# Attention of a two-layer hybrid transformer: three rotating PSUM banks for the turned probabilities, one bank for the weighted values, and the latent turn ahead of the scores

## What is computed

```python
def attend(q, k, v, scale):
    s = jnp.einsum('bqhd,bkhd->bhqk', q, k).astype(jnp.float32) * scale
    p = jax.nn.softmax(s, axis=-1).astype(v.dtype)
    return jnp.einsum('bhqk,bkhd->bqhd', p, v)

ya_x = blocked_attention(qa_x, concat([ka_c, ka_x]), concat([va_c, va_x]), MLA_SCALE)
yb_x = neighborhood_attention(qb_x, kb_x, vb_x, kb_c, vb_c, na_rpb, rows)
if need_ctx:                     # layer 0 only
    ya_c = attend(qa_c, ka_c, va_c, MLA_SCALE)
    yb_c = attend(qb_c, kb_c, vb_c, NA_SCALE)
```

## Time and profile before

| what | value |
|---|---|
| median of 3 runs | 2893.85 us (2892.34 to 2894.07) |
| the profiled execution | 2889.44 us, its span 2887.6 us |
| PE busy | 2807.2 us (97%) |
| DVE busy | 1482.7 us (51%) |
| ACT busy | 947.4 us (33%) |
| POOL busy | 263.3 us (9%) |
| PE in the chain that ended last | 89% |
| granted TensorE clock, mean | 0.996 of full speed |

### The profile page before, as it was taken

The page is one execution under the profiler, slowest core; times in us unless marked ns, Lnnn a source line. Parts: engine busy times, 40 slices in busy tenths (PEclk is TensorE's granted clock), DMA queues, the critical chain, the costliest instruction groups (busy, mean ns, idle before and its releaser), DMA issues.

```text
span 2887.6 us, 42480 instructions
## 1 busy us (share of the span) xinstructions
PE 2807.2 (97%) x16327; PEld 2646.7 (92%) x16327; DVE 1482.7 (51%) x2293; ACT 947.4 (33%) x1526; POOL 263.3 (9%) x279
## 2 busy tenths in 40 slices
PE   7999999999988899999999999999999998999999
PEld 5999999989977789999999999999998987888887
DVE  6554355455477665533553555245346587633332
ACT  3221122233388642211222322112224388532231
POOL 1000000031234210000000100000003234000000
PEclk9999999999999999999999999999999999999999
DMA  6433243223100224322442234133223201233333
GB/s 224 135 122 99 82 137 122 82 63 78 32 14 12 79 74 134 124 85 81 137 133 58 88 117 134 55 123 117 72 65 87 58 14 46 81 95 107 90 100 90
DMA packets 361092, 262.99 MB, mean 91 GB/s; under 512 B 11086, under 2 KB 339188, under 8 KB 359952
## 3 DMA queue, kind: packets, MB, share of 16 engines
q1 hardware_dynamic: 359440, 256.86, 29.5%
q10 hardware_dynamic: 896, 4.46, 0.4%
q0 software_dynamic: 640, 0.09, 0.0%
HBM read 255.08 MB, written 2.10 MB: 89 GB/s over the span
## 4 chain that ended last, share of the span: by engine, by line
PE 89%; ACT 4%; DVE 3%; issue 2%; POOL 1%; DMA 0%; SPq 0%; POOLq 0%; ACTq 0%; DVEq 0%
PE pair L427 24%; PE pair L428 24%; PE pair L435 24%; PE pair L1311 2%; PE pair L1313 2%; PE pair L1312 2%; PE pair L682 2%; PE pmid L2109 2%; PE pair L683 2%; PE pair L684 2%; ACT prob L2180 1%; ACT pt_hi L2165 1%; DVE pt_lo L2254 1%; PE psum L2134 1%; PE psum L2136 1%
## 5 line engine op out<-in xcount | busy, mean ns | idle before, releaser
L427 PE MATMUL pair<-h_lo,w_hi 128*128 128x384 f32 (+1 forms) x2656 | 906.4, 343 | 0.7 <-ACT sg L1102 0.4
L428 PE MATMUL pair<-h_hi,w_hi 128*128 128x384 f32 (+1 forms) x2656 | 905.4, 343 | 0.0
L427 PEld LDWEIGHTS pair<-h_lo,w_hi 128*128 128x128 f32 x2656 | 498.5, 188 | 22.8 <-issue 0.6
L428 PEld LDWEIGHTS pair<-h_hi,w_hi 128*128 128x128 f32 x2656 | 498.8, 188 | 21.3
L403 DVE TENSOR_TENSOR w_lo<-w_raw,w_hi 128x1024 fp32r<-128x1024 f32 (+1 forms) x262 | 349.0, 1332 | 324.5 <-ACT w_hi L396 321.3
L435 PE MATMUL pair<-h_hi,w_lo 128*128 128x384 f32 (+1 forms) x2656 | 513.8, 343 | 0.0
L435 PEld LDWEIGHTS pair<-h_hi,w_lo 128*128 128x128 f32 x2656 | 463.4, 188 | 20.6
L396 ACT ACTIVATE w_hi<-w_raw 128x1024 fp32r<-128x1024 f32 (+1 forms) x262 | 296.2, 1131 | 539.8 <-PE pair L435 507.4
L427 PE MATMUL pair<-s_lo,w_hi 128*128 128x384 f32 (+1 forms) x1100 | 377.7, 343 | 0.0
L428 PE MATMUL pair<-s_hi,w_hi 128*128 128x384 f32 (+1 forms) x1100 | 377.2, 343 | 0.0
L949 DVE SCALAR_TENSOR_TENSOR pmid<-mod_raw,cs_rows 128x1024 f32<-128x1024 f32 x256 | 315.3, 1232 | 74.8 <-DMA mod_raw<-in_w_mod_rows 58.1
(11 more groups left out here) (310 smaller groups left out, 3603.3 us busy)
## 6 DMA issues: line engine op xcount, KB each, us to landing
mod_raw<-in_w_mod_rows SPq DMA_DIRECT2D x64, 1024.0 KB, 4.9
w_raw<-in_w_ffn_gate SPq DMA_DIRECT2D x88, 512.0 KB, 3.8
w_raw<-in_w_ffn_up SPq DMA_DIRECT2D x88, 512.0 KB, 3.8
w_raw<-in_w_ffn_down SPq DMA_DIRECT2D x64, 704.0 KB, 4.6
w_raw<-in_w_in SPq DMA_DIRECT2D x32, 512.0 KB, 4.0
w_raw<-in_w_out SPq DMA_DIRECT2D x12, 512.0 KB, 4.2
w_raw<-in_w_q_up SPq DMA_DIRECT2D x8, 576.0 KB, 4.1
mod_first<-in_w_mod ACTq DMA_DIRECT2D x4, 1024.0 KB, 9.2
```

Of the source, the lines that this page charges most:

```text
L427: eng.matmul(dst, wh, rl, start=k == 0, stop=False)
L428: eng.matmul(dst, wh, rh, start=False, stop=False)
```

## The change

Five things change, all inside the attention:

1. The turned parts get a running number (`turn_no`) and rotate over three banks: the two of `pmid` and the second of `psum2`. A transposition of number N waits for the subtraction of number N-3. The semaphores of the latent parts are gone; `a_t`, `a_pth` and `a_ptl` count parts.
2. On PE the latent part of chunk s-2 is turned ahead of the scores of chunk s (`turn_part` before `attention_scores`), the context part behind them.
3. The product with the values (`weigh_values`) is made in one piece, in odd steps, in the first bank of `psum2` for every pair. It waits for the output of the pair before (`a_out`).
4. ACT makes the copy of a finished pair behind the exponential of its step instead of ahead of it.
5. DVE makes the `pt_lo` of the latent part of chunk s-2 ahead of the maximum of chunk s, and that of the context part behind it; the sum and the scaling of a pair come after both.

```diff
+        def turn_no(l, c):
+            return ATT_C0[l] + c + latent_parts(l, c)
+
+        TURN_PLACES = [pmid[:, 0:512], pmid[:, 512:1024], psum2[:, 512:1024]]
+
+        def turned_at(number, a, b):
+            return TURN_PLACES[number % 3][:, 0:b - a].rearrange("p (k q) -> p k q", q=P)
...
+        def turn_part(eng, l, c, m):
+            keys = chunk_info(l, c)[4]
+            a, b = keys[m]
+            number = turn_no(l, c) + m
+            eng.wait_ge(a_exp, ATT_C0[l] + c + 1)
+            wait_if(eng, a_ptl, number - 2)
+            for k in range(a // P, b // P):
+                last = eng.transpose(turned_at(number, a, b)[:, k - a // P, :], prob[:, c % 3, k * P:(k + 1) * P], ident[:, :])
+            last.then_inc(a_t, 1)
+
+        def weigh_values(eng, l, b):
...
+            wait_if(eng, a_out, c0 // 2 + b)
+            eng.wait_ge(a_rsum, c0 + 2 * b + 2)
+            for h in range(2):
+                eng.transpose(psum2[:, (2 + h) * P:(3 + h) * P], stat[:, (2 * b + h) % STATS, 2:3].broadcast_to([P, P]),
+                              ident[:, :])
+            eng.wait_ge(a_ptl, turn_no(l, 2 * b + 2))
+            both = psum2[:, 0:2 * P].rearrange("p (c q) -> p c q", c=2)
+            for k in kc:
...
+            last.then_inc(a_pv, 1)
 
         def attention_pe(eng, l):
...
+                parts = len(chunk_info(l, s - 2)[4]) if 2 <= s < n + 2 else 0
+                if parts == 2:
+                    turn_part(eng, l, s - 2, 0)
                 if s < n:
...
+                    attention_scores(eng, l, s)
+                if parts:
+                    turn_part(eng, l, s - 2, parts - 1)
+                if s >= 5 and s % 2:
+                    weigh_values(eng, l, (s - 5) // 2)
...
# attention_act
-                if s >= 5 and s % 2 and s < n + 4:
-                    b = (s - 5) // 2
...
-                    eng.activation(y_f[...], psum2[other, bank:bank + 2 * P], ACT.Copy).then_inc(a_copied, 1)
                 if s < n:
...
                     eng.wait_ge(a_max, c0 + s + 1)
-                    wait_if(eng, a_t, c0 + s - 2)
+                    if s >= 3:
+                        eng.wait_ge(a_t, turn_no(l, s - 2))
                     eng.activation(prob[:, s % 3, a:b], pair[s % 2][:, a:b], ACT.Exp, ...).then_inc(a_exp, 1)
+                if s >= 5 and s % 2 and s < n + 4:
+                    b = (s - 5) // 2
...
+                    eng.activation(y_f[...], psum2[other, 0:2 * P], ACT.Copy).then_inc(a_copied, 1)
...
# attention_dve
+                parts = len(chunk_info(l, s - 2)[4]) if 2 <= s < n + 2 else 0
+                if parts == 2:
+                    turned_lo(eng, l, s - 2, 0)
                 if s < n:
                     a, b = chunk_info(l, s)[4][0][0], TOK
                     eng.wait_ge(a_s, c0 + s + 1)
                     eng.tensor_reduce(stat[:, s % STATS, 0:1], pair[s % 2][:, a:b], AX_X, ALU.max, negate=True).then_inc(a_max, 1)
+                if parts:
+                    turned_lo(eng, l, s - 2, parts - 1)
                 if s >= 6 and s % 2 == 0:
...
-                if 2 <= s < n + 2:
-                    c = s - 2
...
-                        eng.tensor_tensor(pt_lo[...], pmid[...], pt_hi[...].bitcast(F32), ALU.subtract)\
-                           .then_inc(a_latent_lo if a < SEQ else a_ptl, 1)
```

More of the change, by code:

```diff
@@ new lines, in turn_part @@
+        def turn_part(eng, l, c, m):
[8 more added lines that the diff above has]
+        def weigh_values(eng, l, b):
+            c0 = ATT_C0[l]
+            kind, i, j, q0, keys = chunk_info(l, 2 * b)
+            tiles = [[k for k in range(TOK // P) if k >= SEQ // P or 0 <= k - near(kind, x)[0] < near(kind, x)[1]]
+                     for x in (q0, q0 + P)]
+            kc = sorted(set(tiles[0] + tiles[1]), key=lambda k: (k >= SEQ // P, not all(k in t for t in tiles), k))
+            wait_if(eng, a_out, c0 // 2 + b)
[4 more added lines that the diff above has]
+            eng.wait_ge(a_ptl, turn_no(l, 2 * b + 2))
+            vals = v_both[:, :, 2 * i + j, :] if kind == "mla" else vn_both[i][:, :, j, :]
+            both = psum2[:, 0:2 * P].rearrange("p (c q) -> p c q", c=2)
+            for k in kc:
+                c1, c2 = [h for h in range(2) if k in tiles[h]][0], [h for h in range(2) if k in tiles[h]][-1] + 1
+                dst, slots = both[:, c1:c2, :], slice(2 * (b % 2) + c1, 2 * (b % 2) + c2)
+                ph, pl = pt_hi[:, k, slots, :], pt_lo[:, k, slots, :]
+                first, end = k == kc[0], k == kc[-1]
+                if first:
+                    eng.matmul(dst, vals[:, k, :], ph, start=True, stop=False)
+                last = eng.matmul(dst[0:V_DIM], vals[:, k, 0:V_DIM], pl, start=False, stop=False)
+                if not first:
+                    last = eng.matmul(dst, vals[:, k, :], ph, start=False, stop=end)
+            last.then_inc(a_pv, 1)
@@ L2083, in attention_pe @@
[L2083 to L2090, removed]
@@ L2221, in attention_pool, with turned_lo @@
                        .then_inc(y_lo_done, 1)
+        def turned_lo(eng, l, c, m):
+            kind, _, _, q0, keys = chunk_info(l, c)
+            a, b = keys[m]
+            number, d = turn_no(l, c) + m, moved(kind, q0, a)
+            eng.wait_ge(a_pth, number + 1)
+            eng.tensor_tensor(pt_lo[:, (a + d) // P:(b + d) // P, c % 4, :], turned_at(number, a, b),
+                              pt_hi[:, (a + d) // P:(b + d) // P, c % 4, :].bitcast(F32), ALU.subtract).then_inc(a_ptl, 1)
         def attention_dve(eng, l):
```

120 lines of the change are left out of this document (37 added, 83 removed).

## The result

The changed kernel takes 2998.51 us (median of 4 runs, 2995.64 to 3001.15) against 2893.1 us beside it: a ratio of 1.0366, with a 95% interval of 1.0348 to 1.0384. It is 3.7% slower. The profiled execution spans 2996.3 us against 2887.6, 108.7 us more.

What follows compares the result with a forecast made beforehand. PE was taken to bound the kernel (89% of the chain), with ACT and DVE nearly as full, so their order decides. Terms 35 + 28 + 2.5 + 9.5 + 8 = +83 us gave 2976 us, range 2944 to 3008.

Steps and rivals of the forecast that it cites:

- 5 for POOL: Attention: stalls for POOL's `lo` halves, counted at nothing in the sum, +5 us at the range's upper end.
- The loop of `pt_hi`, `pt_lo`, maximum, exponential: ACT and DVE, full MLA step: these four follow one another without overlap, 3.10 us a step against 2.63.
- Layer 1's MLA stretch: Eight heads of four chunks, each step in the serial loop, plus copies: 118 us against 82.8, +35 us.
- the sign to look for: Changed profile, layer 1's MLA: exponentials should start 3.1 to 3.9 us apart.
- Copies of ACT inside the loop: ACT's copies between exponential and next `pt_hi` lengthen the loop: pair copy .40 every second step, `ks_hi` .74, `qs_hi` .54.
- Rival A: Attention: the loop costs only its bare 3.10 us a step, copies and context steps hidden; 2919 us, chance .07.
- Layer 0's MLA: Two full loops and an 11.4 us context chain a head: 144.4 us against 116.75, +28 us.
- The clock: PE in layer 0's attention: pauses waiting for `a_out` lower its clock; +8 us, bounds 0 and 20.
- NA: The two NA stretches: longer steps and context chain, +2.5 us in layer 1 and +9.5 us in layer 0.
- The bound on PE's busy share: MLA stretches: PE busy for about 65 to 70%; prediction wrong if still over 90% in layer 1's.
- B: Rival, attention faster: freed banks help and the maximum is not held back; 2880 us, chance .04.
- C: Rival: PE's clock stays at 1.2 GHz for most of the attention; 3070 us, chance .04.

Runs made afterwards that it cites:

- e1: Changed kernel with DVE making the maximum of chunk s first, both subtractions of chunk s-2 and the pair's sum behind it: 2929.0 us.
- e2: Kernel before with DVE's latent `pt_lo` of chunk s-2 put ahead of the maximum of chunk s, nothing else: 2959.4 us.
- e3: Changed kernel with each latent part turned twice by PE, extra work that changes no result: 2987.3 us.
- e6: e4 with PE's latent turn put back behind the scores of its step; three turning banks, one value bank: 2903.3 us.
- e9: e6 with the second bank of `psum2` given back to the value product, so two value and two turning banks: 2911.6 us.
- e4: Changed kernel with DVE's whole order of before: maximum, sum and scaling of the pair, then both subtractions: 2911.4 us.
- e7: Kernel before with PE's latent turn of chunk s-2 moved ahead of the scores of chunk s, nothing else: 2960.5 us.

## Why the prediction held

The forecast was 2976 us in a range of 2944 to 3008, and slower with .94; measured were 2998.5, 105 us slower for 83 forecast. The mechanism held. That the time lies inside the range is in part luck: the terms named for its upper end (clock at 20, 5 for POOL, 4 for NA) add up to +104, or 2998 us, and not to the 3008 that stands there, and those of the lower end to +56 and not +50. No term among them is the one that was missed by most. Step by step:

**The loop of `pt_hi`, `pt_lo`, maximum, exponential** was priced at 3.10 us a step. Measured is 3.10. Layer 1's MLA stretch was put at 118 us and took 119.85. e1 (taking it away) and e2 (adding it alone) show the cause: -69 and +66 us. Once the loop runs, the exponentials there start 3.10 to 4.68 us apart and not 3.1 to 3.9 as the sign to look for said; a step with a pair copy and `ks_hi` costs 4.24 by the forecast's own prices, so that sign was stated too narrowly. In the reading ahead of it, the transposes' 20.8 us were the largest wait of PE in layer 0, not of all engines: DVE waited 21.3 us for `pt_hi`.

**Copies of ACT inside the loop** were counted fully. The timeline shows the output copy between the exponential and `pt_hi`, and the step longer by its .52 us. Rival A, the bare loop at 2919 us, is out by that and by the time.

**Layer 0's MLA** was put at 144.4 us without the clock and took 155.87. e3, with the clock at .97 there, took 147.93. So the chain through context chunks, with PE's product on it, was right within some 4 us, and at least 8 us are the clock's.

**The clock** was mis-sized at +8 us, between bounds of 0 and 20. The mean clock of .981 over 2996 us against .996 over 2888 is about 114 us at half speed against 23. Not all of it costs: in layer 1's MLA PE is off the loop. At least 11 us are shown, net of the work that e3 adds, 8 of them in layer 0's MLA. The page on the clock gate that was weighed (the Trainium skill, TensorE: Matmul & The Clock Gate, section "A second HAM failure mode: psum-queue depth-cycling") fits the trace in that the clock swings in a kernel that cycles banks with short pauses (.96 and 1.66 us in the stretch of 1.16 us of work shown under e3). But banks as such are not the cause: e6 rotates over the same three at a mean clock of .995, and e2, with the banks of before, has .986.

**NA** was put at +2.5 and +9.5 us, and it was +5.6 and +14.8, at clocks of .90 that I had priced only once, in a common term. In e3 layer 1's NA had a clock of 1.00 and was 1 us shorter, so most of the excess there is not the clock; in layer 0 e3's clock was .89, and the cause of the 5 us stays open.

**The ends** were left out, and this is the step that failed by most, 12 us for 0. I took the stretch behind the last exponential as unchanged, and gave it no term. There the last products come one behind the other through the single value bank, with nothing left to do beside them. The timeline of PE at the end of layer 0's attention:

```profile
1040.12 0.43 PE L2121 MATMUL psum<-ident,stat 128*128 128x128 f32 x2 [1.81 <-DVE y_f L2272]
...
1043.05 0.69 PE L2121 MATMUL psum<-ident,stat 128*128 128x128 f32 x2 [1.38 <-DVE y_f L2272]
...
1044.39 0.63 PE L1411 MATMUL pair<-h_lo,wo_hi 128*128 128x512 f32 x1
```

The output projection starts 6.9 us behind the last exponential (1037.51); before it was 3.6 (987.43 behind 983.80). In layer 1 it is 9.4 us against 4.3. It starts at the lower clock, too: its matmul of 512 columns takes .63 us there. e6 and e9, which differ in the banks alone, show that it is the value bank. The projection's first matmul in layer 0, in e6 (one value bank, last exponential at 985.77) and in e9 (two, 988.91):

```profile
992.25 0.63 PE L1411 MATMUL pair<-h_lo,wo_hi 128*128 128x512 f32 x1
993.14 0.50 PE L1411 MATMUL pair<-h_lo,wo_hi 128*128 128x512 f32 x1 [0.40 <-DVE wo_lo L2272]
```

That is 6.5 us against 4.2, and in layer 1 8.2 against 5.3.

**The bound on PE's busy share** was a smaller miss: 65 to 70% of the MLA stretches forecast, 75.5 and 75.7% measured. At the lower clock the same matmuls are busy for longer, and I had not thought of that.

**Rivals B and C.** For B, the right order on DVE was thought to leave 2880 us with the other parts kept. e4 is that kernel and took 2911: the value bank and the turn ahead of the scores are dearer than the 5.5 us a pair that I gave them (layer 1's MLA has 5.8), and the larger part of B, 18 us won in layer 0, did not come at all: its MLA took 121.7 us for 116.75 before. For C, the clock did fall, but in layer 0's MLA only for some 3 to 10 us at a time, and came back by itself. That half speed fills PE's pauses, and so raises the clock again, is my reading and was not tried. (C's 5.07 us of PE's work a pair stands in no row; 79.30 us for 15.75 pairs are 5.03, which changes nothing.)

## What to carry to other kernels

Here three engines were each 85 to 96% full and passed one chunk around, and a serial loop between two of them cost more (66 us alone, e2) than the wait that the third bank was to remove (20.8 us). Before moving an instruction in an in-order engine, follow from it to the engine that needs it and back, and add up the starts: if the way back ends at the same step's instruction, the sum is the new step time. Here one subtraction ahead of one maximum made 2.63 us into 3.10 and more. A reorder on one engine and the number of banks behind it are one decision: the turn ahead of the scores costs 8 us with three banks, 84 with two and 68 with one latent bank of its own.

## What the runs showed of the hardware that was not expected

More work made the kernel faster. The doubled transposes of e3 (some 39 us of PE time) took 11 us off, as the granted clock in layer 0's MLA rose from .87 to .97. The falls outlast the attention: with the clock low at the end of layer 0's attention, a 512-column matmul of the output projection took .63 us against .39 to .50 in the kernel before. And an idle PE alone did not bring the clock down. In e7's layer 1 MLA PE was less busy than in the changed kernel's (82.34 of 117.23 us against 90.70 of 119.85), and the clock there was 1.00 against .93. Why, no run here shows.
